# Recurrence and neighbourhood attention in eight joint steps, two heads at a time, turned by transposes; output weights of the attention beside the heads' mean

## What is computed

```python
a_lat = neighbourhood_attention(nh(na_q), nh(na_k), nh(na_v), nh(cna_k), nh(cna_v), rpb)
g_lat, g_ctx = hgrn2_mixer(hg_q, (hg_ff, hg_fb), hg_i, hg_g,
                           chg_q, (chg_ff, chg_fb), chg_i, chg_g, lb, hg_norm_w, with_ctx_out)
y = jnp.concatenate([a_lat.reshape(b, s, NA_WIDTH), g_lat], axis=-1) @ w_out
```

## Time and profile before

| | us |
|---|---|
| median of 3 runs | 2149.23 |
| lowest, highest | 2144.33, 2150.7 |
| span of the profiled execution | 2148.6 |

### The profile page before, as it was taken

One profiled execution on the slowest core, in us unless ns is written; L12 is line 12 of the kernel. 1 busy time (PEld: TensorE's weight loads), 2 busy tenths in 40 slices (PEclk: granted clock), 3 DMA queues, 4 the chain that ended last, 5 costly groups with the idle time before them and its releaser, 6 DMA issues.

```text
span 2148.6 us, 40333 instructions
## 1 busy us (share of the span) xinstructions
PE 2098.7 (98%) x16798; PEld 2026.0 (94%) x16798; DVE 1561.3 (73%) x2758; ACT 1122.7 (52%) x1745; POOL 263.1 (12%) x256
## 2 busy tenths in 40 slices
PE   7999999999999999999999999999998999999998
PEld 7899999999999999999999999999878999999998
DVE  6877688774998777876777677573455887877764
ACT  5567678545444666654444454563245554445553
POOL 0000000002887544410000000000000000000000
PEclk9999999999999999999999999999999999999999
DMA  5543433667555444447777777322103777654553
GB/s 191 168 131 119 151 118 117 206 207 246 187 187 177 141 145 138 139 156 245 234 238 275 241 252 249 118 90 99 35 25 128 259 243 245 236 195 169 185 183 122
DMA packets 104293, 375.43 MB, mean 175 GB/s; under 512 B 11568, under 2 KB 12208, under 8 KB 103728
## 3 DMA queue, kind: packets, MB, share of 16 engines
q1 hardware_dynamic: 104112, 372.86, 51.7%
HBM read 370.71 MB, written 2.10 MB: 174 GB/s over the span
## 4 chain that ended last, share of the span: by engine, by line
PE 75%; DVE 17%; ACT 4%; issue 2%; DMA 1%; POOL 0%; SPq 0%; DVEq 0%; ACTq 0%
PE ps L376 20%; PE ps L377 19%; PE ps L378 19%; DVE wl L1559 3%; PE ps L779 3%; DVE arenap L1901 2%; ACT wh L1103 1%; DVE arena L1702 1%; PE ps L573 1%; DMA raw<-in_ada 1%; PE ps L462 1%; DVE arenap L1866 1%; PE ps L463 1%; PE ps L464 1%; PE ps L877 1%
## 5 line engine op out<-in xcount | busy, mean ns | idle before, releaser
L376 PE MATMUL ps<-xah,wh 128*128 128x256 f32 x2800 | 798.9, 285 | 5.2 <-POOL wl L2287 2.5
L377 PE MATMUL ps<-xal,wh 128*128 128x256 f32 x2800 | 788.1, 281 | 0.0
L378 PE MATMUL ps<-xah,wl 128*128 128x256 f32 x2800 | 787.6, 281 | 0.0
L1103 ACT ACTIVATE wh<-raw 128x1024 fp32r<-128x1024 f32 (+1 forms) x608 | 620.7, 1036 | 304.0 <-PE ps L378 142.7
L1559 DVE TENSOR_TENSOR wl<-raw,wh 128x1024 fp32r<-128x1024 f32 (+2 forms) x548 | 645.0, 1198 | 179.5 <-ACT wh L1103 178.2
L376 PEld LDWEIGHTS ps<-xah,wh 128*128 128x128 f32 x2800 | 529.0, 189 | 16.0 <-issue 6.1
L377 PEld LDWEIGHTS ps<-xal,wh 128*128 128x128 f32 x2800 | 529.1, 189 | 0.5 <-issue 0.2
L378 PEld LDWEIGHTS ps<-xah,wl 128*128 128x128 f32 x2800 | 529.0, 189 | 0.0
L376 PE MATMUL ps<-hh,wh 128*128 128x256 f32 x1024 | 290.0, 283 | 6.6 <-DVE wl L1559 4.9
L377 PE MATMUL ps<-arenar,wh 128*128 128x256 f32 x1024 | 287.9, 281 | 0.0
L378 PE MATMUL ps<-hh,wl 128*128 128x256 f32 x1024 | 287.8, 281 | 0.0
(11 more groups left out here) (353 smaller groups left out, 3137.1 us busy)
## 6 DMA issues: line engine op xcount, KB each, us to landing
raw<-in_pu SPq DMA_DIRECT2D x128, 512.0 KB, 3.3
raw<-in_pv SPq DMA_DIRECT2D x128, 512.0 KB, 4.0
raw<-in_ada SPq DMA_DIRECT2D x96, 512.0 KB, 4.4
raw<-in_ff_up SPq DMA_DIRECT2D x88, 512.0 KB, 4.2
raw<-in_w_xbc SPq DMA_DIRECT2D x32, 512.0 KB, 3.2
raw<-in_ff_down SPq DMA_DIRECT2D x32, 512.0 KB, 4.0
raw<-in_w_z SPq DMA_DIRECT2D x16, 512.0 KB, 3.3
raw<-in_w_so SPq DMA_DIRECT2D x16, 512.0 KB, 4.2
```

Source lines behind the costliest of these rows:

```text
L376: mm(o, w0, x0, start=start, stop=False, skip_group_check=skip)
L377: mm(o, w0, x1, start=False, stop=False, skip_group_check=skip)
L378: return mm(o, w1, x0, start=False, stop=stop, skip_group_check=skip)
L1103: put(W.hi(i), W.raw(i), ACT.Copy).then_inc(S["high"], 1)
```

## The change

- The second query tile is moved ahead of the `nv` rows. The recurrence's loop and the attention become one loop of eight steps on all engines; its products are now 12 groups (key tile 3 and the two gate tiles). The low halves of these units go to POOL (`W.kinds = "G"`), those of the first eight output units to POOL and DVE in turn.
- An item m is now two heads and one half of the queries. The scores of the two heads are issued alternately, 256 keys each time, into two banks, on rows 0 to 63 and 64 to 127 of the array; so are the state products of the two directions (other rows, other banks) and the values of the two heads (other output rows).
- DVE adds the bias within PSUM and no longer copies; the maximum and the exponential read PSUM. DVE scales the exponentials themselves (`normalised`), and `turned` is a transpose against the identity.
- The output weights' attention half comes first, beside `head_mean` and `head_rows`, then the recurrence half; the last `eo` tile lies in two banks, one for each half, and is read by halves.
- The bias table is two DMAs, the first quarter earlier.

```diff
-        nS, nP = view(ar2, 80, 3, 512), view(ar2, 86, 3, 512)
-        nT = [ar2[:, o * 256:o * 256 + 512] for o in (0, 2, 104)]
-        nD, nst = view(sc2, 7.5, 3, 128), view(sc2, 5, 3, 4)
+        nP, nT, nst = view(ar2, 80, 4, 512), [ar2[:, o * 256:o * 256 + 512] for o in (88, 90, 0, 2)], view(sc2, 5, 4, 4)
...
-        VROWS, QUARTERS, HEADS = (0, 3, 6, 9), [("ek", 3), ("eq", 1), ("hg", 0), ("hg", 1)], range(20, 36, 2)
+        VROWS, QUARTERS = (0, 3, 6, 9), [("ek", 3), ("hg", 0), ("hg", 1)]
...
+            tile(("eq", 1), "ev_q", 2, 8, XA, l0)
+            def scored(m):
+                j, qt = m // 2, m % 2
+                P = [take(("ns", 2 * m + a)) for a in range(2)]
+                t.wait_ge(*B.is_empty(("eq", j // 2)))
+                t.wait_ge(*B.is_empty(("ek", j)))
+                for c in range(2):
+                    for a in range(2):
+                        b = slice(64 * a, 64 * a + 64)
+                        last = mm(P[a][:, 256 * c:256 * c + 256], nq[b, j, qt * 128:qt * 128 + 128], nk_[b, j, 256 * c:256 * c + 256],
+                                  start=True, stop=True)
+                        if c:
+                            last.then_inc(B.full(("ns", 2 * m + a), len(W.units)), 1)
+
+            def turned(m):
+                for n in (2 * m, 2 * m + 1):
                     P = take(("nt", n))
-                    i = n % 3
-                    t.wait_ge(S["n_diag"], n + 1)
+                    t.wait_ge(S["n_norm"], n + 1)
                     for k in range(4):
-                        last = mm(P[:, k * 128:k * 128 + 128], nP[:, i, k * 128:k * 128 + 128], nD[:, i, :], start=True, stop=True)
+                        last = tp(P[:, k * 128:k * 128 + 128], nP[:, n % 4, k * 128:k * 128 + 128], ident)
                     last.then_inc(B.full(("nt", n), len(W.units)), 1)
 
-                def scored(n):
-                    h, qt = n // 2, n % 2
-                    j, b0 = h // 2, 64 * (h % 2)
-                    P = take(("ns", n))
-                    t.wait_ge(*B.is_empty(("eq", 1)))
-                    t.wait_ge(*B.is_empty(("ek", 3)))
-                    mm(P[:, :], nq[b0:b0 + 64, j, qt * 128:qt * 128 + 128], nk_[b0:b0 + 64, j, :], start=True, stop=True).then_inc(
-                        B.full(("ns", n), len(W.units)), 1)
-
-                def valued(n):
-                    h, qt, i = n // 2, n % 2, n % 3
-                    b0 = 64 * (h % 2)
-                    P = B[("nav", n // 4)] if n % 4 else take(("nav", n // 4))
-                    t.wait_ge(*B.is_empty(("nt", n)))
-                    t.wait_ge(*B.is_empty(("nv", 3)))
+            def valued(j):
+                P = take(("nav", j))
+                t.wait_ge(*B.is_empty(("nv", 3)))
+                for qt in range(2):
+                    for a in range(2):
+                        t.wait_ge(*B.is_empty(("nt", 4 * j + 2 * qt + a)))
                     for k in range(4):
-                        last = mm(P[b0:b0 + 64, qt * 128:qt * 128 + 128], nv[:, k, h * 64:h * 64 + 64],
-                                  nT[i][:, k * 128:k * 128 + 128], start=k == 0, stop=k == 3)
-                    if n % 4 == 3:
-                        last.then_inc(B.full(("nav", n // 4), len(W.units)), 1)
-                    else:
-                        last.then_inc(S["n_part"], 1)
-                for n in range(19):
-                    if n < 16:
-                        scored(n)
-                    if 2 <= n < 18:
-                        turned(n - 2)
-                    yield
-                    if n >= 3:
-                        valued(n - 3)
-                    yield
+                        for a in range(2):
+                            h, n = 2 * j + a, 4 * j + 2 * qt + a
+                            last = mm(P[64 * a:64 * a + 64, qt * 128:qt * 128 + 128], nv[:, k, h * 64:h * 64 + 64],
+                                      nT[n % 4][:, k * 128:k * 128 + 128], start=k == 0, stop=k == 3)
+                last.then_inc(B.full(("nav", j), len(W.units)), 1)
 
...
+            def state_products(n):
+                P = [take(("sd", n, d)) for d in range(2)]
+                for h in range(4):
                     for d in range(2):
-                        c = n if d == 0 else 7 - n
-                        tt, r = c // 4, 32 * (c % 4)
-                        if n < 7:
-                            P = take(("sd", n, d))
-                            for h in range(4):
-                                last = mm(P[:, h * 128:h * 128 + 128], kdt[r:r + 32, d * 8 + h * 2 + tt, :],
-                                          hv[r:r + 32, tt, h * 128:h * 128 + 128], start=True, stop=True)
+                        tt, r = chunk(n, d) // 4, 32 * (chunk(n, d) % 4)
+                        last = mm(P[d][:, h * 128:h * 128 + 128], kdt[r:r + 32, d * 8 + h * 2 + tt, :],
+                                  hv[r:r + 32, tt, h * 128:h * 128 + 128], start=True, stop=True)
+                        if h == 3:
                             last.then_inc(B.full(("sd", n, d), len(W.units)), 1)
-                        t.wait_ge(*B.is_empty(("sd", n - 1, d) if n else ("s0", d)))
-                        for h in range(4):
-                            o = (h % 2) * 256 + 32 * c
-                            last = mm(O[h // 2][:, o:o + 32], SS[:, d, n % 2, h, :], QE[:, d, h * 256 + 32 * c:h * 256 + 32 * c + 32],
-                                      start=False, stop=n == 7 and d == 1, skip_group_check=True)
-                            if n == 7 and d == 1 and h % 2:
-                                last.then_inc(B.full(("o", h // 2), len(W.units)), 1)
-                        if n < 7 or d == 0:
-                            last.then_inc(S["o_part"], 1)
-                        yield
-
+
...
+                if n == 9:
+                    next(nv_rows)
+                    t.wait_ge(S["ld_b0"], 16)
+                    scored(0)
+                if n == 13:
+                    turned(0)
+                    scored(1)
+            W.kinds = "G"
+            twelve = (step for key in QUARTERS for step in
+                      (quarters(key, "ev_k", key[1], (XA, XC)) if key[0] == "ek" else quarters(key, "ev_hg", 2 * key[1])))
+            for n in range(8):
+                if n < 7:
+                    state_products(n)
+                if n % 2:
+                    valued(n // 2)
+                next(twelve)
+                if n < 7:
+                    turned(n + 1)
+                state_outputs(n, 0)
+                if n < 6:
+                    scored(n + 2)
+                if n % 2 == 0:
+                    next(twelve)
+                state_outputs(n, 1)
+            W.kinds = "VG"
...
-            def mixer_out(i, part, halves=(0, 1)):
-                P = take(("eo", i)) if part else B[("eo", i)]
-                for half in halves:
+            def mixer_out(i, part):
+                for half in range(2):
+                    key = (("eo", i), half) if i == 3 else ("eo", i)
+                    P = B[key] if part or (half and i < 3) else take(key)
+                    o = P[:, 0:256] if i == 3 else P[:, half * 256:half * 256 + 256]
                     u, hi, lo = unit(("eo", i, half, part), "ev_out", 2 * i + half, 512 * part, 512, 128)
                     for q in range(4):
                         k = 4 * part + q
                         cat(k)
-                        last = product(P[:, half * 256:half * 256 + 256], hi[:, q, :], lo[:, q, :], XC[0][:, k, :], XC[1][:, k, :],
-                                       k == 4 and half == 0, k == 3, skip=True)
-                    if part or half == 0:
+                        last = product(o, hi[:, q, :], lo[:, q, :], XC[0][:, k, :], XC[1][:, k, :],
+                                       k == 0 and (half == 0 or i == 3), k == 7, skip=True)
+                    if part and (half or i == 3):
+                        last.then_inc(B.full(key, len(W.units)), 1)
+                        W.done[u] = B.is_full(key)
+                    else:
                         last.then_inc(W.used(u), 1)
-                    yield
-                if part == 0:
-                    last.then_inc(B.full(("eo", i), len(W.units)), 1)
-                    W.done[u] = B.is_full(("eo", i))
...
-            heads = (step for i in range(4) for step in mixer_out(i, 1))
-            for n, _ in enumerate(neighbourhood()):
-                if n == 3:
-                    head_mean()
-                if n == 7:
-                    head_rows()
-                if n in HEADS:
-                    next(heads)
-            run(heads)
...
+            mixer_out(0, 0)
+            head_mean()
+            mixer_out(1, 0)
+            head_rows()
+            mixer_out(2, 0)
+            mixer_out(3, 0)
+            W.kinds = "V"
+            for i in range(4):
+                mixer_out(i, 1)
...
+            def biased(m):
+                j, qt = m // 2, m % 2
+                for a in range(2):
```

(50 more changed lines are left out.)

299 lines of the change are left out of this document (118 added, 181 removed).

## The result

The median of four runs is **2103.4 us** (2098.2 to 2104.4), beside 2149.3 us for the kernel before (2144.3 to 2150.7): the ratio is 0.978 with a 95% interval of 0.977 to 0.980, so 45.9 us faster. I had forecast 2115.9, in a range of 2099 to 2134.

A forecast was written before the change was run, and what follows sets the result against it. PE, busy for 98% of the span, was the bound. The changed stage's 191.1 us became 154.3 + 1.2 + 1.3 + 6.3 = 163.1, 28.0 less; with 5.3 for pairs, 2149.2 - 33.3 = 2115.9 us, range 2099 to 2134.

The forecast's parts named there:

- PE is the bound: Whole kernel: PE busy for 98% of the span, so the change is worth what it takes off PE's line.
- Unit prices: PE's small matmuls: 0.114 us an instruction of states, 0.22 of scores, 0.106 of values, about 0.17 a change of shape.
- Two heads at a time: Paired scores, states and values, 40.5 us of PE: side by side saves between 0 and 20.3; 5.3 taken, scores only.
- The prediction's own sign of being wrong: Loop on PE: forecast is wrong if state products or values come much closer than 0.1 us.
- The rival's 2103.9: Paired products fully side by side: half of 40.5 us goes, scores-to-turns chain shows some 3 us more; chance 0.20.
- Turns by transposes: Attention turns on PE: 0.103 us a transpose, 0.82 for eight; half clock would cost 6.6 more, not added.
- The wait for the squares and the half clock behind it: Attention before the change: PE stands 2.08 us behind ACT's squares, then runs at clock 0.50; 7.9 us lost there.
- Waits in the loop: Scores-to-turns chain in even steps: PE waits 0.3 us in four steps, 1.2 in all.
- POOL, the bias's DMAs at nothing; 1.3 for the eighth output unit: POOL's low halves and bias DMAs cost nothing; ACT's late high half of the eighth output unit costs 1.3 us.
- The tail, 6.3: Last output product to first feed-forward tile: 6.3 us with the last tile ended by halves, against 10.6 before.
- The chain opens: Rival in the loop: turns come 1.5 us late in all eight steps, 2133.2 us; chance 0.08.
- the clock falls: Rival in the loop: waits of some 2 us at the turns bring half clock; at five places 2160.7 us; chance 0.07.

## Why the prediction was right, and where it was off

- **PE is the bound, so the change is worth what it takes off PE's line.** Right: stage 46.3 less, span 45.9 less.
- **Unit prices** (0.114 an instruction of states, 0.22 of scores, 0.106 of values, 0.17 a change of shape). Right. With the pairs kept apart, (1.98 - 0.17) / 16 = 0.113, (1.92 - 0.17) / 8 = 0.22, (3.25 - 0.17) / 32 = 0.096, one meeting of two runs included.
- **"Two heads at a time", taken at 5.3: the term that failed.** The bounds (0 and 20.3) were right, the choice between them was not. All of the upper bound came: the 19 groups take 23.9 us, and without 0.17 each for the change of shape 20.7 remain, about half of 40.5. The argument was that new weights every 0.1 us are near a floor, since 32 columns come no faster than 128. There is such a pace, but for one set of rows or columns, not for the engine: in the changed kernel eight pairs of L951 come every (1.09 - 0.17) / 8 = 0.115 us, an instruction of each direction in each. The prediction's own sign of being wrong, state products or values much closer than 0.1 us, came: 1.09 / 16 = 0.07 and 1.90 / 32 = 0.06. That the time still lies in the range is owed to the range's reaching down to the rival's case, not to the forecast's mechanism. The mechanism that the Trainium skill gives (TensorEngine Tiling (Array Packing), Key Properties: separate tiles load and multiply in parallel) is what the trace shows, at 1.09 us against 1.98.
- **The rival's 2103.9, hit within 0.5 us: in part by luck.** With full overlap the forecast would have been 28.0 + 20.3 off, 2100.9. The rival added 3 us for a chain from scores to turns that would then show. It hardly does: the waits for the norms are 1.4 us, against 1.2 forecast without it. What makes up the difference is mostly the tail, 1.7 us longer than forecast.
- **That it is the order in turn that does it.** So the prediction called it ("alternately"), and wrong for the most part: the order is worth 6.2 of these 20 us, the rest comes with the pair being near each other.
- **Turns by transposes, 0.103 an instruction.** Nearly: 0.109 in a run of eight (three of the seven groups in the loop); the other four take 1.05 to 1.06 us, three of them behind a wait. Against products they save some 7 us. The Trainium skill's rule (TensorE: Matmul & The Clock Gate, Part 4) that the full clock doesn't engage for transposes is not borne out here, where they come eight at a time between other matmuls: 1.00 in all windows of the loop, and in the kernel with products too. Longer stretches of transposes alone no run shows. It was right to leave out the 6.6.
- **The wait for the squares and the half clock behind it, 7.9 us in all.** Right. It doesn't come back in the changed kernel, and it does where the mean is left bare.
- **Waits in the loop, 0.3 in four steps.** 0.48 in three, and 0.36 once for ACT, ahead of scores: 1.8 against 1.2.
- **POOL, the bias's DMAs at nothing; 1.3 for the eighth output unit.** Right for the first two within the loop; the third came as a wait of 0.61 before the eighth unit, for POOL's low half and not for ACT's high half.
- **The tail, 6.3.** It is 8.0. A low half of 1.2 us stands between the two halves' residuals on DVE as forecast, but DVE comes to it at 1.6 us behind the last product and not at 0.9: its sums start only 0.1 behind that product, after a wait of 0.48 for ACT's square of the tile before, and with the first half take 1.5. So the last square ends at 3.6 and not 3.0. From there the norm takes 4.3 us and not 3.3, with the clock at 0.50, which I had not put in. That clock seems to go with the execution rather than the kernel: the one with the values' order undone has the same tail, the same two waits and the clock at 1.00, and takes 6.8 us from start to start instead of 8.1. So a difference of one or two us between two traces can lie in such a stretch alone.

```profile
1594.11 0.28 PE L376 MATMUL ps<-xch,wl 128*128 128x256 f32 x1
1595.63 0.58 PE L481 MATMUL ps<-J,sc 128*128 128x1 f32 x4 [1.23 <-DVE sc L1580]
...
1597.91 0.61 PE L481 MATMUL ps<-J,sc 128*128 128x1 f32 x4 [0.81 <-ACT sc L1113]
...
1600.89 0.39 PE L518 MATMUL ps<-xah,wh 128*128 128x256 f32 x1 [0.22 <-ACT xah L1144]
```

- **The chain opens, the clock falls.** Neither happened. The second is real all the same: with the pairs kept apart the clock fell, which cost some 11 us, and no wait stood ahead of the first fall.

## What to carry to other kernels

Where a group of small matmuls uses only a half or a quarter of the array's rows or columns, put beside it the same work of another head or direction on the other rows or columns: here it was nearly free (16 instructions in 1.09 us, where eight alone took 1.09), and runs of four needed no change of order. Runs of eight and more were better put in turn. And an unknown price between 0 and a bound isn't to be set by the pace of instructions that all used the same rows: such rows say nothing on what a second set can do at the same time.

## What the runs showed of the hardware that I had not expected

- Matmuls on different rows overlap even when they are issued as runs, not in turn: 1.07 us for four and four score instructions (1.92 on the same rows), 1.64 for eight and eight of states (1.98), each meeting of two runs giving back some 0.31 to 0.38.
- The granted clock can fall to 0.50 with PE busy for the whole window. With the pairs kept apart it has a mean of 0.89 from 1500 to 1560 and 0.83 from 1560 to 1600, against 1.00 and 0.95 in the changed kernel. Groups on a part of the array without partners don't always bring it: the kernel before has them at 1.00 from 1565 to 1620.
- A turn of float32 by the transpose is one instruction a block and by a product two: 0.87 us against 1.78 for eight blocks.
